# First weight block of five output projections split inside the stage in front of it, in a buffer of its own

## What is computed

```python
mix = jnp.concatenate([a_out, b_out, c_out], axis=-1) @ w_out[l]      # first block
x = x + g1 * mix
...
return jnp.concatenate([hm, ha], axis=-1) @ w_out                     # odd mixer
...
return jnp.einsum('bhsm,bmhd->bshd', p, v).reshape(B, S, XA_WIDTH) @ wo  # cross-attention
```

## Time and profile before

| | us |
|---|---|
| median of 3 runs | 2665.19 (2662.9 to 2672.44) |
| the profiled execution's own time | 2661.47 |
| its span | 2659.8 |
| PE busy | 2298.5 (86%) |
| DVE busy | 1855.4 (70%) |
| ACT busy | 1336.7 (50%) |
| granted TensorE clock, mean | 0.924 of full |

### The profile page before, as it was taken

One profiled execution on the slowest core, in us unless ns is written; L12 is line 12 of the kernel. 1 busy time (PEld: TensorE's weight loads), 2 busy tenths in 40 slices (PEclk: granted clock), 3 DMA queues, 4 the chain that ended last, 5 costly groups with the idle time before them and its releaser, 6 DMA issues.

```text
span 2659.8 us, 30674 instructions
## 1 busy us (share of the span) xinstructions
PE 2298.5 (86%) x11133; PEld 1890.3 (71%) x11133; DVE 1855.4 (70%) x1946; ACT 1336.7 (50%) x1430; POOL 55.9 (2%) x130
## 2 busy tenths in 40 slices
PE   3836899784689999999999999987679999686998
PEld 3725788673578787878787878767567878575786
DVE  7877676677588887888788888865644446555553
ACT  2413334342267776777677777753334435343443
POOL 2000000000000000000000000000000000000000
PEclk9956999896799999999999999998789999898999
DMA  8730578550169999999999999994224554222453
GB/s 299 277 135 1 196 287 312 197 168 1 48 237 346 340 341 318 349 344 344 315 346 341 345 350 345 341 327 147 85 85 147 185 173 144 95 96 79 144 188 134
DMA packets 412855, 595.17 MB, mean 224 GB/s; under 512 B 20315, under 2 KB 327750, under 8 KB 412742
## 3 DMA queue, kind: packets, MB, share of 16 engines
q1 hardware_dynamic: 407040, 586.55, 64.0%
q10 hardware_dynamic: 5702, 7.04, 0.8%
HBM read 592.47 MB, written 1.05 MB: 223 GB/s over the span
## 4 chain that ended last, share of the span: by engine, by line
PE 70%; DVE 11%; DMA 4%; ACT 4%; issue 3%; POOL 0%; SPq 0%; DVEq 0%; ACTq 0%; POOLq 0%
PE bank L136 21%; PE bank L137 21%; PE bank L138 20%; DMA ring<-in_moe_w_up 3%; DVE ring_rounded L685 2%; DVE ring_rounded L291 1%; PE bank L2530 1%; PE bank L2511 1%; PE bank L2490 1%; PE bank L1725 1%; DMA ring<-in_ffn_w_down 1%; PE bank L1187 1%; ACT PT_rounded L282 1%; DVE AT L1625 1%; PE bank L490 1%
## 5 line engine op out<-in xcount | busy, mean ns | idle before, releaser
L136 PE MATMUL bank<-ring_rounded,hT_rounded 128*128 128x512 f32 (+3 forms) x944 | 376.8, 399 | 49.9 <-DVE ring_rounded L291 45.8
L685 DVE TENSOR_TENSOR ring_rounded<-ring,z_rounded 128x2048 fp32r<-128x2048 f32 x148 | 339.0, 2292 | 71.7 <-ACT z_rounded L677 69.8
L136 PE MATMUL bank<-ring_rounded,z_rounded 128*128 128x512 f32 x896 | 363.4, 406 | 9.6 <-issue 6.6
L685 DVE TENSOR_TENSOR ring_rounded<-ring,zT_rounded 128x2048 fp32r<-128x2048 f32 x145 | 332.4, 2292 | 48.4 <-ACT zT_rounded L677 47.4
L136 PE MATMUL bank<-ring_rounded,L_rounded 128*128 128x512 f32 x712 | 286.3, 402 | 16.6 <-DVE score_rounded L818 11.5
L677 ACT ACTIVATE z_rounded<-ring 128x2048 fp32r<-128x2048 f32 x148 | 283.3, 1916 | 32.9 <-DMA ring<-in_moe_w_up 27.5
L677 ACT ACTIVATE zT_rounded<-ring 128x2048 fp32r<-128x2048 f32 x145 | 277.9, 1916 | 41.4 <-DMA ring<-in_moe_w_up 19.7
L136 PEld LDWEIGHTS bank<-ring_rounded,hT_rounded 128*128 128x128 f32 x944 | 183.4, 194 | 87.9 <-issue 54.7
L136 PEld LDWEIGHTS bank<-ring_rounded,z_rounded 128*128 128x128 f32 x896 | 169.4, 189 | 50.1 <-issue 9.1
L137 PE MATMUL bank<-zT_rounded,score_rounded 128*128 128x512 f32 x488 | 194.6, 399 | 0.0
L685 DVE TENSOR_TENSOR ring_rounded<-ring,PT_rounded 128x2048 fp32r<-128x2048 f32 x71 | 162.6, 2290 | 44.1 <-ACT PT_rounded L677 44.1
(11 more groups left out here) (480 smaller groups left out, 4974.3 us busy)
## 6 DMA issues: line engine op xcount, KB each, us to landing
ring<-in_moe_w_gate SPq DMA_DIRECT2D x224, 512.0 KB, 5.1
ring<-in_moe_w_up SPq DMA_DIRECT2D x224, 512.0 KB, 7.0
ring<-in_moe_w_down SPq DMA_DIRECT2D x224, 512.0 KB, 7.9
ring<-in_ffn_w_gate_up SPq DMA_DIRECT2D x88, 512.0 KB, 5.0
ring<-in_ffn_w_down SPq DMA_DIRECT2D x66, 512.0 KB, 7.8
ring<-in_w_ada SPq DMA_DIRECT2D x48, 512.0 KB, 7.0
ring<-in_w_in SPq DMA_DIRECT2D x32, 512.0 KB, 4.9
xn<-in_w_ada SPq DMA_DIRECT2D x24, 512.0 KB, 9.5
```

The source lines that it names most:

```text
L136: pe.matmul(out, r32(a[0]), r32(b[1]), start=start, stop=False, skip_group_check=True)
L685: dve.tensor_tensor(r32(w), w, high(hi), ALU.subtract).then_inc(sem_out, 1)
```

## The change

Two helpers' calls are added, and buffers are given out anew. `splits_ahead` runs `first_split` for the `presplit` blocks of the projection that a stage has under `ahead`: in HGRN on ACT behind the last exponentials and on DVE behind the last masked copies; in the attentions on ACT in front of the exponentials and on DVE behind the copy L1226 of n = 0. `w_out` (twice) and `od_out` take one block ahead, `xa_out` (twice) both of its blocks. `ev_out`, behind the even mixer, is left as it was. `c.AT` and `c.score` become parts of one buffer `c.ats`, so that a whole block fits in it.

```diff
+def splits_ahead(c, eng, st):
+
+    if st is None:
+        return
+    for i in range(st['presplit']):
+        first_split(c, eng, st, i)
...
 def attend_plan(core, a):
-    a['calls'] = []
+    a['calls'], a['ahead'] = [], None
...
             dve.tensor_copy(a['PT'][n][:, 4 * b * P:4 * b * P + w], c.pb[a['turn'][b % 3]][:, 0:w])\
                .then_inc(c.s['att_PT_b'], 1)
+        if n == 0:
+            splits_ahead(c, dve, a['ahead'])
...
 def attend_act(c, act, a):
     H = a['heads']
+    splits_ahead(c, act, a['ahead'])
...
     take(HG_EXPS - 1)
     take(HG_EXPS)
+    splits_ahead(c, dve, st['ahead'])
 
     dve.wait_ge(c.s['hg_square'], 2 * (k + 1))
...
         act.activation(v[:, :, B:2 * B], v[:, :, B:2 * B], ACT.Exp).then_inc(c.s['hg_exp'], 1)
+    splits_ahead(c, act, st['ahead'])
     for n in range(NT):
         act.wait_ge(c.s['hg_out'], 2 * k + n + 1)
...
-        add(proj(c, name, src, waits, tiles, c.hi_out))
+        p = add(proj(c, name, src, waits, tiles, hi))
+        if host is not None:
+            host['ahead'] = p
+            p['presplit'], p['hi_free'] = len(free), free
...
-        add_x(rows_view(t['w_out'][l]), KD, True, c.hsplit, turned_events(tr) + [('att_mixT', 2 * (l + 1))], 'w_out')
+        add_x(rows_view(t['w_out'][l]), KD, True, c.hsplit, turned_events(tr) + [('att_mixT', 2 * (l + 1))], 'w_out',
+              c.hi_out, hg, [('ada_folded', 3 * l + 3)])
...
-            add_x(rows_view(t['od_w_out_2'][0]), KD, False, c.hsplit, turned_events(tr) + [('att_mixT', 8)], 'od_out')
+            add_x(rows_view(t['od_w_out_2'][0]), KD, False, c.hsplit, turned_events(tr) + [('att_mixT', 8)], 'od_out',
+                  c.hi_odd, la['att'], [('proj_done', 2 * last + 2)])
...
-        add_x(rows_view(t['xattn_wo_2'][l]), 4, False, c.hsplit, [('att_mixT', 6 if l == 0 else 10)], 'xa_out')
+        add_x(rows_view(t['xattn_wo_2'][l]), 4, False, c.hsplit, [('att_mixT', 6 if l == 0 else 10)], 'xa_out',
+              c.hi_cross, xs['att'], [('proj_done', 2 * last + 2)] * 2)
...
-        c.AT = shared('AT', [P, NT, B_HEADS, P])
+        c.ats = shared('ats', [P, SLOT])
+        c.AT = c.ats[:, 0:NT * B_HEADS * P].rearrange('p (n h t) -> p n h t', n=NT, h=B_HEADS)
+        c.score = c.ats[:, NT * B_HEADS * P:SLOT].rearrange('p (n s) -> p n s', n=NT)
...
-        c.hi_out = [PTf, zT0, zT1, mixf]
+        c.hi_out, c.hi_even = [adaf, PTf, zT0, zT1], [PTf, zT0, zT1, mixf]
+        c.hi_odd, c.hi_cross = [atsf, PTf, zT0, zT1], [adaf, mixf]
```

More of the change, by code:

```diff
@@ L2879, in feat, with add_x @@
                 for a in range(lo, hi, 512)]
-    def add_x(view, k, gated, src, waits, name):
+    def add_x(view, k, gated, src, waits, name, hi, host=None, free=()):
         tiles = [(view, a, 512, k, 0, 'tok', a if gated else 'add', (lambda n, a=a: c.x[:, n, a:a + 512]))
                  for a in (0, 512)]
-        add(proj(c, name, src, waits, tiles, c.hi_out))
+        p = add(proj(c, name, src, waits, tiles, hi))
+        if host is not None:
+            host['ahead'] = p
+            p['presplit'], p['hi_free'] = len(free), free
         updates[0] += 1
@@ L2911, in make_plan @@
                 st['gmlp'] = stages[-2]
+        hg = stages[-1]
         tr = add(turn_stage(c, number('turn'), [3, 4, 5, 6, 7], [('mix_ready', 4 * (l + 1))]))
-        add_x(rows_view(t['w_out'][l]), KD, True, c.hsplit, turned_events(tr) + [('att_mixT', 2 * (l + 1))], 'w_out')
+        add_x(rows_view(t['w_out'][l]), KD, True, c.hsplit, turned_events(tr) + [('att_mixT', 2 * (l + 1))], 'w_out',
+              c.hi_out, hg, [('ada_folded', 3 * l + 3)])
         h = norm(c.x, lambda kc: c.modA[:, 8 + kc:9 + kc], lambda kc: c.modC[:, 16 + kc:17 + kc], mod=2 * l + 2)
@@ L2929, in make_plan @@
             add(dict(kind='even', evacuated=proj_evacuated(p)))
-            add_x(rows_view(t['ev_w_out_2'][0]), KD, False, c.hsplit, [('ev_mixT', 2)], 'ev_out')
+            add_x(rows_view(t['ev_w_out_2'][0]), KD, False, c.hsplit, [('ev_mixT', 2)], 'ev_out', c.hi_even)
         else:
@@ L2944, in make_plan @@
             p['fill'] = latents_fill(c, od)
-            add(mla_stage(c, proj_evacuated(p)))['mlstm'] = ml
+            last = p['tiles'][-1]['t']
+            la = add(mla_stage(c, proj_evacuated(p)))
+            la['mlstm'] = ml
             tr = add(turn_stage(c, number('turn'), [0, 1, 2, 3], [('mix_ready', 10)]))
-            add_x(rows_view(t['od_w_out_2'][0]), KD, False, c.hsplit, turned_events(tr) + [('att_mixT', 8)], 'od_out')
+            add_x(rows_view(t['od_w_out_2'][0]), KD, False, c.hsplit, turned_events(tr) + [('att_mixT', 8)], 'od_out',
+                  c.hi_odd, la['att'], [('proj_done', 2 * last + 2)])
         h = norm(c.grow, columns('mem_norm_g_2', l), waits=lambda n: [('mem_loaded', 32)], beside=True)
@@ L2954, in make_plan @@
         p = add(proj(c, 'xa_q', c.hsplit, [], feat(rows_view(t['xattn_wq_2'][l]), 0, 512, 0), c.hi_in, h))
-        add(xa_stage(c, proj_evacuated(p)))
-        add_x(rows_view(t['xattn_wo_2'][l]), 4, False, c.hsplit, [('att_mixT', 6 if l == 0 else 10)], 'xa_out')
+        last = p['tiles'][-1]['t']
+        xs = add(xa_stage(c, proj_evacuated(p)))
+        add_x(rows_view(t['xattn_wo_2'][l]), 4, False, c.hsplit, [('att_mixT', 6 if l == 0 else 10)], 'xa_out',
+              c.hi_cross, xs['att'], [('proj_done', 2 * last + 2)] * 2)
         h = norm(c.x, columns('norm_ffn_g_2', l))
@@ L3040, in build @@
         c.sin, c.cos = sb('sin', [P, 96]), sb('cos', [P, 96])
-        c.score, c.sel = shared('score', [P, NT, S]), sb('sel', [P, NT, S])
+        c.sel = sb('sel', [P, NT, S])
         c.work, c.eq = sb('work', [P, S]), sb('eq', [P, S])
@@ L3084, in build @@
         z0, z1 = zf[:, 0:SLOT], zf[:, SLOT:2 * SLOT]
-        c.highs = [PTf, mixf, Lf, zT0, zT1, z0, z1]
+        adaf, atsf = c.ada[:, :], c.ats[:, :]
+        c.highs = [PTf, mixf, Lf, zT0, zT1, z0, z1, adaf, atsf]
         c.hi_in, c.hi_kv = [PTf, mixf, Lf], [Lf, PTf, mixf]
```

## The result

| | before | changed |
|---|---|---|
| median, us | 2668.61 (4 runs) | 2635.80 (4 runs) |
| lowest to highest, us | 2662.90 to 2672.44 | 2631.27 to 2639.61 |
| profiled execution's own time, us | 2661.47 | 2634.75 |
| its span, us | 2659.8 | 2633.0 |

The ratio is 0.9865, 95% interval 0.9846 to 0.9884. The direction and the mechanism were forecast, and the median of 2635.80 lies in the range, but the gain doesn't agree with the sum: it is 26.8 us between the two profiled spans, 32.8 us between the medians, 36 us by the ratio, against 25.3 forecast. The time before that the forecast started from, 2665.19, was a low draw. That the median of 2635.80 falls in the range from 2634 to 2651 is thus in part luck: the measured ratio applied to 2665.19 is 2629.2, under its lower end.

A forecast was written before the change was run, and what follows sets the result against it. PE was taken to wait at five output projections for ACT's and DVE's weight splits; 21.3 + 4.1 - 0.1 = 25.3 us off the profiled 2661.47 gave 2636.2 us (2639.9 against the median), range 2634 to 2651.

The forecast's parts named there:

- The gaps: PE's waits for the weight split at five output projections go, 4.26 to 4.27 us each, 21.3 us in sum.
- What is late next: In w_out and od_out, block 1's split ends while PE is busy with block 0, margin over 1 us.
- the moved work: Splits moved into idle time of ACT and DVE cost 0 in w_out and od_out, 0.1 us in sum in xa_out.
- The clock in xa_out: At both xa_out PE keeps the full clock through the shorter pause: 4.1 us won, 0 if it falls.
- The clock in od_out: At od_out keeping the full clock would win 1.3 us or nothing; taken as 0.
- the bounds: At both w_out the clock's rise may come earlier or later: taken as 0, within -0.8 and 0.8 us each.
- rival e: Routed part: joined buffer and moved places cause access conflicts; 0.25 us more per step loses 28 us; chance 0.03.
- The step to the median: The profiled execution, 2661.47 us, lies 3.7 us under the median of the runs shown, 2665.19.
- (a): At xa_out the clock falls anyway: 21.2 us won, 2644.0; chance 0.22.
- (b): A later stage, routed or dense part, swallows both w_out gains: 16.8 us won, 2648.4; chance 0.10.
- (c): Moved instructions aren't hidden in the attentions, DVE runs late: 14.0 us won, 9.9 with the clock lost; chance 0.07.
- (d): Weights or buffer come so late that ACT takes the splits where it did: no gain, 2665.2; chance 0.03.

The follow-up runs named there:

- i_fill9: The kernel before, no split ahead, plus 9 matmuls of constants on PE while it waits for weights at each xa_out: 2659.64 us, ratio 0.9972.
- b_wout: The changed kernel with only the two w_out taking their block ahead, joined buffer kept, against the kernel before: 2652.58 us, ratio 0.9920.
- a_after: The changed kernel measured again, against the kernel before on the same chip: 2632.93 us, ratio 0.9845.
- g_warm: The changed kernel plus matmuls of constants in PE's waits (20 before turn behind HGRN, 16 before probabilities, 4 at each start): 2633.47 us, 0.9873 of the kernel before.

## Why the prediction was wrong in size

- **The gaps** ("Sum 21.3 us"): right. 21.8 us, since PE follows DVE by 0.06 us and not by 0.15.
- **What is late next, and the moved work**: right. PE starts no block late, the split of block 1 ends while PE is busy, HGRN and MLA hide theirs, and cross-attention gives back 0.13 us against 0.1.
- **The clock in xa_out** ("I take 4.1"): right, 1.9 each by the table; i_fill9 shows apart from the splits that it brings time.
- **The clock in od_out** ("I take 0"): wrong. It was kept, 1.3 us (23.3 to 22.0). I had read the fall 1.9 us behind the last transposes as a sign that it would fall again. The rule of the Trainium skill (TensorE: Matmul & The Clock Gate, "HAM oscillation"), which I had weighed and not followed, was the right one here. Behind it the memory's projection kept its clock too, 1.7 us that I had not looked for.
- **w_out**: means of the table, the eight kernels without its split ahead against the six with it, are 258.9 and 253.5 in W0, 107.6 and 103.1 in W1; 5.4 and 4.5 us for gaps of 4.36, within the steps. `w_out` itself took 23.8 us in layer 0 and 24.0 in layer 1 before, 23.1 to 23.9 and 23.7 to 24.5 in three profiles of the changed kernel: nothing on the whole, as I took, and within the bounds.
- **The places of buffers** (rival e: "the routed part's pace by the joined buffer"): I looked at this for a loss only, and priced it at nothing in the sum. It is a gain of 4 to 6 us. The place I named was right and the sign wrong: the matmuls that read `score` became 9 ns quicker each, in the dense parts as in the routed one.
- **The step to the median** ("That execution lies 3.7 us under the median"): too small, which shifts the time forecast, not the gain. 87 further executions of the kernel before have a mean of 2669.6, 8.1 above the profiled one. It was a quick one, with a mean clock of 0.924 against 0.921 over the 87; among these time and clock go together (correlation -0.66, 1.4 us for 0.001 of clock).

So: 21.8 + 3.8 + 1.3 + 1.7 - 0.1 = 28.5, and some 5 of the places, 33 to 34 us. Measured are 35.2 between the means of 14 executions of the changed kernel (2634.4) and the 87, and 35 to 41 by the three ratios, whose intervals are 5 to 6 us to either side. The step of the prediction that failed is the sum of terms outside the five gaps: it had no term for places (some 5 us), none for what a shift does to the clock elsewhere (1.7), and took `od_out`'s at 0 (1.3). What stays open is in what way the place of `score` acts, and whether the 1 or 2 us that are left are anything. By such a sum b_wout should gain 8.7 + 5.7 = 14.4 us, and its interval begins at 15.2: the excess of that part is not accounted for.

The rivals: (a) fell with the clock rows of both `xa_out`. (b) fell with W0 and W1 in the whole: b_wout gained 21 us, so the stages behind `w_out` don't swallow its gap; single profiles can't show this, since the routed stage alone varies from 1189 to 1203 us. (c) and (d) fell with the timelines above. (e) fell: no kernel with the joined buffer was slower, and its matmuls were quicker.

## What to carry to other kernels

Where the first weight block of a product is prepared when its activations are complete, prepare it in idle time of the stage in front, in a buffer that this stage leaves free; count the rows of idleness ahead of each moved instruction, as they foretold every cost here within 0.1 us. Where a pause of TensorE of 5.8 us became one of 1.5, it was worth its length and, at three of the five places, the clock behind it. Where a buffer that matmuls read is moved, compare the distance between their starts before and after. And for a kernel with dozens of pauses of a few us, take the baseline from many executions: one profile and three runs were 8 and 4 us off here, the first nearly a quarter of the gain.

## What the hardware showed that I had not expected

- The clock's fall depends on more than the length of the pause: behind the same 2.72 us of idleness it was granted at 0.50 in one kernel and at 1.00 in the other, and went with what PE had done before it. Behind the norm in the stage od profiles of one and the same kernel differ in this way (0.50 in two, 1.00 in a_after).
- The Trainium skill (TensorE: Matmul & The Clock Gate, "Part 1: The HAM clock gate") says the number of matmuls at the low clock varies between runs of one kernel. The steps of the table agree: in W1 two profiles of the kernel before differ by 3.1 us, and three of the changed one by 3.0. Over the program the time lost at the low clock is 113 to 126 us of some 2650, over 4%.
- Moving a 2 KB buffer next to another, with the same instructions, changed the time by 0.2% in three groups of runs out of three. From the start of each of the 712 matmuls that read it to the next start it is 227 ns at the new place (twelve profiles) and 236 at the old one (six).
- Keeping TensorE at full clock by idle work (g_warm, mean clock 0.941 against 0.928) gave no time that could be measured, though the start that it served ran at the full pace.
